# A Strassen form for the second output projection, and expert pairs that alternate between group halves

## The reference, cut to what matters

```
x = x + concat([y_pool, y_attn]) @ w_out[l]            # 512x1024 @ 1024x1024: the second output projection
h = rmsnorm(x, xattn_norm[l])
x = x + memory_cross_attention(h, mem, ...)            # starts with h @ w_q, 1024 -> 512
h = rmsnorm(x, ffn_norm[l])
x = x + hierarchical_moe(h, ...)                       # 4 groups of 8 experts, FF 256

g_sel = argmax(h @ wg_router + bg_router)              # each token takes ONE group of the four
top_v, top_i = top_k(e_logits of that group, 2)        # and two experts inside it
for g in range(4):
    hid = silu(h @ w_gate[g]) * (h @ w_up[g]) * gates
    out = out + hid @ w_down[g]
```

## Time and profile before

| | us |
|---|---|
| median of 3 runs (1506.1 to 1508.77) | 1506.77 |
| the profiled execution, own time | 1508.07 |
| its span in the trace | 1506.3 |
| PE busy | 1405.1 (93%) |
| DVE busy | 840.2 (56%) |
| ACT busy | 424.5 (28%) |
| POOL busy | 56.4 (4%) |

### The profile page before, as it was taken

How to read it: one execution, slowest core, us unless ns; L and a number is a source line. 1 busy time by engine, 2 the same in 40 slices (tenths; PEclk the granted TensorE clock), 3 DMA queues, 4 the chain that set the end, 5 groups by cost and what they waited for, 6 DMA issues and landing times. The chain is left out here.

```text
span 1506.3 us, 14765 instructions
## 1 busy us (share of the span) xinstructions
PE 1405.1 (93%) x5258; PEld 776.8 (52%) x5258; DVE 840.2 (56%) x1858; ACT 424.5 (28%) x694; POOL 56.4 (4%) x114
## 2 busy tenths in 40 slices
PE   7999999999999999999999999999899786899975
PEld 3455555555555558888887444445444433333321
DVE  5567677776776747767476449955333413221211
ACT  2445344453444415101112143133302330000000
POOL 0000000000000000000000000000000001122211
PEclk9999999999999999999999999999999996999998
DMA  7131111312110114232332211010124468999994
GB/s 288 29 112 56 42 56 38 103 57 70 57 42 23 39 51 168 84 109 87 108 141 87 83 50 56 15 67 26 43 70 180 145 271 334 404 408 408 407 404 146
DMA packets 38057, 201.96 MB, mean 134 GB/s; under 512 B 6880, under 2 KB 8800, under 8 KB 31072
## 3 DMA queue, kind: packets, MB, share of 16 engines
q1 hardware_dynamic: 30688, 186.29, 33.1%
q0 software_dynamic: 4608, 8.40, 2.3%
q10 hardware_dynamic: 2688, 6.29, 1.1%
HBM read 196.77 MB, written 12.58 MB: 139 GB/s over the span
## 5 line engine op out<-in xcount | busy, mean ns | idle before, releaser
L449 PE MATMUL gla_proj<-hT,weight_slots 128*128 128x512 f32 x864 | 379.5, 592 | 1.9 <-DVE hT L815 1.9
L449 PEld LDWEIGHTS gla_proj<-hT,weight_slots 128*128 128x128 f32 x864 | 160.8, 190 | 188.3 <-issue 187.6
L2987 PE MATMUL moe_banks<-weight_slots,moe_room 128*64 128x512 f32 x400 | 91.9, 608 | 9.9 <-DMA weight_slots<-in_w_gu 7.4
L1756 PE MATMUL mid_p_proj<-hT,weight_slots 128*128 128x512 f32 x208 | 93.0, 594 | 1.8 <-PEq L170 1.8
L3139 DVE SCALAR_TENSOR_TENSOR moe_room<-moe_banks,moe_kept,moe_room 128x256 f32<-128x256 f32 x16 | 7.7, 484 | 124.2 <-ACT moe_room L3094 124.2
L606 ACT ACTIVATE gla_level_decay<-gla_level_decay 128x1024 f32<-128x1024 f32 x56 | 58.9, 1055 | 46.0 <-DVE gla_level_decay L735 45.6
L1756 PEld LDWEIGHTS mid_p_proj<-hT,weight_slots 128*128 128x128 f32 x208 | 39.1, 190 | 52.1 <-issue 52.1
L2987 PEld LDWEIGHTS moe_banks<-weight_slots,moe_room 128*64 128x64 f32 x400 | 29.0, 140 | 64.4 <-issue 53.0
L475 PEld LDWEIGHTS gla_level<-gla_level_q,gla_level_k 128*128 128x128 f32 x448 | 55.0, 192 | 11.5 <-issue 11.5
L570 ACT COPY gla_raw<-gla_proj 128x512 f32<-128x512 f32 x38 | 22.4, 589 | 123.0 <-PE gla_proj L449 123.0
L1578 PE MATMUL rn_p_out<-y2T,weight_slots 128*128 128x512 f32 x128 | 55.2, 593 | 1.5 <-PEq L170 1.5
(11 more groups left out here) (478 smaller groups left out, 2410.7 us busy)
## 6 DMA issues: line engine op xcount, KB each, us to landing
weight_slots<-in_w_gu SPq DMA_DIRECT2D x25, 2048.0 KB, 23.0
weight_slots<-in_w_dn SPq DMA_DIRECT2D x11, 2048.0 KB, 33.2
weight_slots<-in_w_gla SPq DMA_DIRECT2D x40, 512.0 KB, 3.6
weight_slots<-in_w_merge SPq DMA_DIRECT2D x32, 512.0 KB, 4.2
weight_slots<-in_w_out SPq DMA_DIRECT2D x16, 512.0 KB, 4.0
weight_slots<-in_w_v SPq DMA_DIRECT2D x3, 2048.0 KB, 7.6
hT<-in_w_gu SPq DMA_DIRECT2D x3, 2048.0 KB, 34.9
weight_slots<-in_w_u SPq DMA_DIRECT2D x8, 512.0 KB, 5.5
```

What stands on the lines that cost most here:

```text
L449: last = nc.tensor.matmul(pj[:, n % 2, :], lhsT, rhs, start=(k == 0), stop=(k == KT - 1))
L1756: last = nc.tensor.matmul(pw[:, n % 2, :], a, b, start=(k == 0), stop=(k == KT - 1))
L2987: last = nc.tensor.matmul(pG[rows, e, :], hgT[:, k, rows], core.as_gate_up(at[k // 4])[:, x, k % 4, :], start=(k == 0), stop=(k == KT - 1))
```

## The change

Five things, with the diff cut to their core:

- The projection stage is written anew. For each pair u of output tiles PE makes 7 products of 4 matmuls of 128x256: x_first, x_second, z_first, z_second, z_third, y_first, y_second. DVE forms 4 weight sums per pair and, once, 4 sums of activations of 1024 columns; the residual is folded in by 256-wide operations. All 8 weight tiles stand in slots 0 to 7. ACT now forms `hT`.
- 7 of the 8 tiles of `hT` are normalised at the end of this stage (`OUT2_SCALED`), behind the second lead product, and only the last in the cross attention.
- Pair u holds experts of groups 0 and 1 when u is even and of groups 2 and 3 when it is odd. So a scatter only waits for the one two pairs back (`step_first`).
- The last pair's `w_dn` comes in two transfers of its output halves, `down` waits for each half apart, and ACT may copy the first half once it is done.
- At the end PE turns the last hidden rows before `down` of pair 14.

```
+OUT2_SCALED = 7
+def residual_norm_stage(core, name, src, room, weight, scale, rs1, ahead, lead, rs):
...
+                for j in range(4, KT):
+                    sp.dma_start(core.W[:, j, :], w[j]).then_inc(core.w_in[j], 16)
...
+                x_first(0)
+                x_first(1)
+                x_second(0)
+                z_first(0)
+                y_first(0)
+                z_second(0)
+                for u in range(1, U):
+                    if u > 1:
+                        x_first(u)
+                    z_first(u)
+                    z_third(u - 1)
+                    y_second(u - 1)
+                    y_first(u)
+                    x_second(u)
+                    z_second(u)
+                follow(0, 0, 2)
+                z_third(LAST)
+                follow(0, 2, 3)
+                y_second(LAST)
+                follow(0, 3, KT)
+                follow(1, 0, 2)
+                pe.wait_ge(acc_done, KT)
+                nc.tensor.matmul(pa[:], core.ones[:], acc, start=True, stop=True).then_inc(sum_ready, 1)
+                follow(1, 2, KT)
...
+                def z_first(u):
+                    pe.wait_ge(formed, 2)
+                    pe.wait_ge(summed, 4 * u + 2)
...
+                scale_tiles(0)
+                sum_second(0)
+                sub(src[:, 0:H, Q:T], src[:, 0:H, Q:T], src[:, H:KT, Q:T]).then_inc(formed, 1)
+                dve.wait_ge(formed, 1)
+                sub(own[:, 0], src[:, 0:H, 0:Q], src[:, 0:H, Q:T]).then_inc(formed, 1)
+                sum_first(0)
+                dve.wait_ge(formed, 2)
+                sub(own[:, 1], src[:, H:KT, Q:T], own[:, 0]).then_inc(formed, 1)
+                second(0)
+                sum_fourth(0)
+                sub(own[:, 2], src[:, H:KT, 0:Q], own[:, 0]).then_inc(formed, 1)
+                sums_ahead(1)
+                third(0)
+                for u in range(1, U):
+                    scale_tiles(u)
+                    second(u)
+                    rest(u - 1)
+                    if u < LAST:
+                        sums_ahead(u + 1)
+                    third(u)
+                    for x in range(2):
+                        squares(2 * (u - 1) + x)
...
+                nc.vector.tensor_tensor(lead[0], pX[:, 0, :], rs, ALU.mult)
+                for k in range(OUT2_SCALED):
+                    dve.wait_ge(lead_read, k + 1)
+                    nc.vector.tensor_tensor(hT[:, k], hT[:, k], rs, ALU.mult)
+                dve.wait_ge(lead_read, KT)
+                nc.vector.tensor_tensor(lead[1], pX[:, 1, :], rs, ALU.mult)
...
-                        if h == 2:
-                            pe.wait_ge(h_ready, k + 1)
+                        if h == 2 and k >= OUT2_SCALED:
+                            pe.wait_ge(h_ready, k - OUT2_SCALED + 1)
...
-                for k in range(KT):
+                for k in range(OUT2_SCALED, KT):
                     nc.vector.tensor_tensor(hT[:, k], hT[:, k], rs1, ALU.mult).then_inc(h_ready, 1)
...
+        def step_first(u, stored, last):
+            gather(u + 4, 1)
+            y_is_out(0, stored)
+            scatter(u + 1, 0)
+            if not last:
+                gather(u + 5, 0)
+            y_is_out(1, stored)
+            if last:
+                pool.wait_ge(y_free, u + 3)
+            scatter(u + 2, 1)
+            chain.restart()
...
             scatter(0, 0)
+            gather(4, 0)
+            scatter(1, 1)
             chain.restart()
-            with pool.Fori(0, PAIRS // 2 - 2) as i:
-                step(pool.snap(i * 2 + 1), pool.snap(i * 16 + 16), True)
-            step(PAIRS - 3, first_out - 16, False)
+            with pool.Fori(0, PAIRS // 2 - 3) as i:
+                step_first(pool.snap(i * 2 + 1), pool.snap(i * 16 + 16), False)
+            step_first(PAIRS - 5, first_out - 32, True)
+            y_is_out(0, first_out - 16)
+            pool.wait_ge(y_free, PAIRS - 1)
+            scatter(PAIRS - 2, 0)
+            y_is_out(1, first_out - 16)
+            pool.wait_ge(y_free, PAIRS)
+            scatter(PAIRS - 1, 1)
             y_is_out(0, first_out)
-            pool.wait_ge(y_free, PAIRS + 1)
-            scatter(PAIRS - 1, 1)
...
         def down(u, e, at, w):
-            pe.wait_ge(place_in[at], w)
             pe.wait_ge(hT_done, u + 2)
-            pe.wait_ge(ya, u + 1)
-            pe.wait_ge(yb, u + 1)
             for half in range(2):
+                if half or isinstance(u, int) and u == PAIRS - 1:
+                    pe.wait_ge(place_in[at] if half else core.last_half, w if half else 16)
+                else:
+                    pe.wait_ge(place_in[at], w)
+                pe.wait_ge((ya, yb)[half], u + 1)
...
-    arr["w_gu"] = np.ascontiguousarray(gu.reshape(2, 2, EPG, 2, KT // 2, P, 2 * FF).transpose(0, 2, 5, 3, 1, 4, 6)).reshape(
+    arr["w_gu"] = np.ascontiguousarray(gu.reshape(2, 2, EPG, 2, KT // 2, P, 2 * FF).transpose(2, 0, 5, 3, 1, 4, 6)).reshape(
```

357 lines of the change are left out of this document (188 added, 169 removed).

## The result

The changed kernel took 1499.57 us in the median of 4 runs (1498.53 to 1502.83), the kernel before 1507.47 us beside it (1506.1 to 1508.77, 4 runs). The ratio is 0.9947, 95% interval 0.9935 to 0.9958. A second group of runs gave 1501.41 against 1508.28 us, ratio 0.9958, interval 0.9942 to 0.9973. So it is faster by about 7 to 8 us, half a per cent.

What follows compares the result with a forecast made beforehand. PE bounds the projection stage, the weight transfers the expert stage. Stage 5.4 plus tail 3.7 gives 9.1 us: the profiled 1508.07 becomes 1499.0 us, the median 1497.7 us, range 1494 to 1502.5.

Steps and rivals of the forecast that it cites:

- The products: Projection stage: 224 records of 256 columns at 0.216 us take 48.4 us instead of 55.0, 6.6 us less.
- no fixed toll shows per record: Projection stage matmuls: 216 against half of 430 ns shows no fixed cost per matmul; with one, 0.6 us less gain.
- DVE at the start: Projection stage's start: PE waits for DVE's sums, 0.8 us at z_first(1) and 0.2 before z_third(0); 1.0 us lost, bounds 0 to 3.
- The end of the stage: Projection stage's end: `hT` scaling is moved, not hidden, DVE about 2 us behind PE; 9.94 us, 0.2 more than before.
- Stage in all: Projection stage: -6.6 + 1.0 + 0.2 = -5.4 us, so the weight stream starts 5.4 us earlier.
- The middle: Expert stage with alternating pairs and freed scatters: PE runs ahead of an already full stream, 0 us; bounds -3 to +10.
- the 4.1% of the rival: Expert stage: paired scatters stretch the 220 us weight stream; 4.1% eats both gains, 6% gives 1510.9 us; chance 0.05.
- the middle that gives more: Expert stage: PE ahead frees places earlier and dry engines get work, 3 us more, 1494.7 us; chance 0.08.
- The tail: End of the expert stage: last scatter issued 3.9 us earlier, 0.2 given back for overlapping scatters; -3.7 us, bounds -5 to +1.
- the wait of 0.88 us at 1491.07: Before the last `down` product in the kernel before: taken as PE waiting 0.88 us for the last weights.
- the turn of pair 15 ahead of `down(14)`: End of the expert stage: the turn falls into PE's 3.14 us wait for `w_dn`, 0 us.

Runs made afterwards that it cites:

- e: Changed kernel with another order of DVE's first steps in the projection stage and 5 instead of 7 `hT` tiles scaled at its end; 1496.96 us, ratio 0.9928.
- a: Kernel before with only the new projection stage, the expert stage left old; 1504.73 us, ratio 0.9979 to before.
- changed_again: The changed kernel, unaltered, timed again in a second group of runs; 1501.41 us, ratio 0.9958 to before.
- m: Kernel before with additional unread matmuls in PE's waits of sparse attention and ahead of the last two `down` products; 1507.73 us, ratio 0.9997.
- k2: Changed kernel with unread matmuls in PE's waits of sparse attention, at the projection stage's end and ahead of the last two `down` products; 1499.81 us, ratio 0.9942.
- c: Changed kernel with POOL's old scatter order, each scatter waiting until the one before has landed; 1506.06 us, ratio 0.9985 to before.
- d: Changed kernel with the last `w_dn` in one whole transfer instead of two halves; 1500.5 us, ratio 0.995 to before.
- g: Changed kernel with 4 and 8 unread matmuls in PE's two waits ahead of the last two `down` products; 1500.26 us, ratio 0.995 to before.
- k: Changed kernel with unread matmuls in PE's waits in sparse attention, at the projection stage's end and ahead of the last two `down` products; 1497.25 us, ratio 0.9935.

## Why the prediction came out

The sign was right, and so was the size of the stage's gain; the tail's came out only where the clock was held. Its steps, in its order:

- *The products.* 224 records at 0.216 us less the old 128 at 0.430. In the trace the steady round from 1097.65 to 1109.74 takes 12.09 us, the blend stage's to the hundredth. Right. Only the remark that no fixed toll shows per record was too coarse: 55.01 us for 128 records are 429.8 ns each, 12.09 for 56 are 215.9, and twice 215.9 is 431.8, so 2 ns per record do show (0.5 us in 224). The term was priced by rows of the right width and holds it already.
- *DVE at the start.* 1.0 us in one wait of z_first(1) and a small one of z_third(0), 0.8 and 0.2 (the prediction's own terms, 11.3 - 10.4, give 0.9 for the first). Measured 0.91 at z_first(1) (0.75 of it as idle) and 0.14 at z_third(0). Right, and kernel e, which takes back 1.14, shows that the order of DVE's first steps is the cause.
- *The end of the stage.* From the ones matmul to the next stage's first matmul 7.94 + 0.28 = 8.22 us were expected, 1145.56 - 1137.32 = 8.24 were measured, with DVE 1.8 us behind PE. Right.
- *Stage in all* -5.4 expected, -5.25 measured in the changed kernel, the same within 0.01 in kernels a and changed_again.
- *The middle.* 0 expected. The stream took 215.6 against 215.4 us, and with the old waits 215.5. Right in the main: the largest value of the ten profiles with the new order, 216.45 us, is a stretch of 0.5%, far from the 4.1% of the rival; the middle that gives more has no trace either.
- *The tail.* -3.9 at the last scatter's issue and +0.2 behind it expected, -2.2 and +0.15 measured: this is the term that was mis-sized. With the clock held the issue comes 3.64 us earlier (m against k2). What the step left out is that the new order of PE leaves two short idle stretches right ahead of the two products on the path, and that the clock then falls, in each of the six profiles of the changed tail where nothing fills them, and in none of the five where matmuls do. It costs 1.7 us on the two products (2.8 in c, about 1.3 in d). The prediction had the wait of 3.14 us into which it put the turn, and reckoned the products behind it at 3.65 us each.
- *Inside the tail* one reason was incomplete although the sum with the clock held was right. The prediction took the wait of 0.88 us at 1491.07 for the arrival of the last weights alone. In kernel a the wait at this place stands against DVE's copy of the turned hidden rows, and in before that copy ends at 1490.89, 0.18 us ahead of the product:

```profile
1490.48 0.41 DVE L3144 COPY moe_room<-moe_banks 128x256 f32<-128x256 f32 x1
```

```profile
1488.58 3.65 PE L3091 MATMUL moe_banks<-weight_slots,moe_room 128*64 128x512 f32 x16 [0.81 <-DVE moe_room L3225]
```

  (the first is before, the second a). In m too the copy ends 0.18 us ahead of the product (1490.43, 1490.61). The profile names the transfer in before and in m, where the copy was done 0.18 us earlier; so the copy alone would explain nearly all of the wait, and how early the last weights were there is not shown. To let the last product follow at once it takes the turn of pair 15 ahead of `down(14)`, which the prediction had at 0, and, with the clock held, the halves as well (the wait of PEld in g). And without the freed scatters nothing of it reaches the end: in c, whose 32 records took 2.8 us over 7.1, the last scatter comes 15.48 us after the start of these products (1497.35 - 1481.87), so 12.7 without the drop, which is before's 12.67 (1498.84 - 1486.17). How the gain would divide with the freed scatters and PE's old order was not run; as an estimate from the rows, the last scatter would be 1.3 us later than with both (0.44 us for the turn and 0.88 of wait).

The prediction's 1497.7 us then sits 1.9 us low in the first group and 3.7 in the second. 1.5 is the tail's clock. What is left has the size of the drops in sparse attention, at the cross attention's start and at the first expert products, which each execution has anew; for the medians this is argued and not shown. Kernel k is at 1497.25 us, but that it meets the forecast is in part luck: k also lacks the 1.9 us of drop in sparse attention that the kernel before has. With the clock held in both kernels the change is worth 7.9 to 8.1 us (m against k2), not 9.1.

The 2.5 us by which the first profile was ahead when the projection stage began made its single time (1498.53) look as if the prediction's sum of 1499.0 had been beaten. It was chance: in a, e, g, c, d and the changed kernel again the stage begins between 1080.9 and 1082.1.

## What to carry to other kernels

Where a stage waits for one engine and the next for a transfer, add the gain of the first at its own boundary and count at the end only what stands behind the last transfer; here the stage's sum held to 0.15 us, and the tail's to 0.3 us once the clock was held, but was 1.7 us too large where it was not. Before you price a matmul by its row, look at what TensorE did just ahead of it: on a path with waits of 1 to 3 us the same product costs 3.65 or 5.35 us, and a few matmuls into a spare bank in such a wait are the cheaper product. Fill only waits that a timeline shows at that very instruction; nine matmuls at a place without a wait cost 2.2 us.
